# The opening of a hybrid encoder block: latent columns first, one token tile at a time, then the recurrent x branch over all tokens

## The chip, the core and the metric

The kernel runs on one core of a Trainium2 chip. The metric is device time in microseconds (us) of one execution. The engines are TensorE (PE; PEld is its weight load), VectorE (DVE), ScalarE (ACT), GpSimd (POOL) and SyncE (SP), which issues most of the DMAs. A line number such as L475 is a line of the kernel before.

## The reference

One encoder block over 512 tokens of width 1024, in float32. What matters here is its opening:

```python
h = rmsnorm(x, norm1_g)
proj = h @ w_in                    # 1024 x 3488
q_a, kv_a, k_rope_raw = ...        # the first 256 + 128 + 32 = 416 columns: "latent columns"
lru_x, lru_y = ...                 # the next 512 + 512 columns
gate_logits = ...                  # the last 2 x 1024 columns
attn = mla_mixer(q_a, kv_a, k_rope_raw, ...) @ w_o_attn      # both latents go through an RMS norm first
rec = rglru_bidir(lru_x, ...)      # 4-tap convolution, gates from 128x128 blocks, two scans
rec = (gelu(lru_y) * rec) @ w_o_lru
```

The rest (gates, output projection, second norm, SwiGLU of width 2816, last norm) follows and keeps its code but for semaphore counts.

## The kernel before, in words

Every engine has its own instruction list, written out by hand; semaphores order them. Products are made to nearly float32 precision from halves: an operand is rounded to `hi` by ScalarE (`split_hi`, L309) and VectorE subtracts to get `lo` (`split_lo`, L319); `product` (L475 to L477) then issues three matmuls, `lo*hi`, `hi*lo`, `hi*hi`. Weights arrive in two raw buffers (pairs of tiles, `raw`, slots p % 2) and are split into four slots of `w_hi` and `w_lo` (tile t in slot t % 4). A slot is free again when TensorE has counted the tile in `w_used`.

The tiles in order are T_X (four tiles of 128 columns of the recurrent x branch), T_A (four tiles, each two of the eight k-blocks of the 416 latent columns), T_G0 (gate weights of direction 0, two tiles), T_Y (four tiles of 128 columns of the y branch), T_V (values), T_G1 (gates of direction 1), and then the heads.

The opening: SyncE loads token tiles 0 and 1 of x (128 tokens x 1024 each), the first pair of T_X, token tiles 2 and 3, the second pair of T_X, eight small parameter rows, and only then, when slots are free, the latent columns. Tokens are normed in two halves of 256: ScalarE and VectorE make sums of squares, POOL takes the power -1/2 (L616), VectorE scales the rows (L1135), TensorE transposes them (`transpose_half`, L1628), ScalarE and VectorE write `hT_hi` (L729) and `hT_lo` (L1114). For each half of tokens TensorE runs all four T_X tiles with 256 moving columns (`half_tile`). Before that it issues 30 transposes of the identity (L1660) that nothing reads. The second half's 16 transposes come between.

Then follow the latent product (96 matmuls, weights are 128 tokens of `hT`, the moving operand is 416 columns of `w`, token tiles 0 to 3 inside each k-block, into PSUM banks 4 to 7), the convolution on VectorE beside it, the gates of direction 0 (`lru_gates`), two y tiles, 16 transposes of the normed latents (L1711), two more y tiles, the values, the gates of direction 1, `q_and_k(0, 0)` and the loop over heads.

Of the kernel before, what the change touches and what calls it, by code (L numbers as in the profile page):

```python
# [32 lines left out]
P = 128  # L33
ALU = mybir.AluOpType
# [25 lines left out]
T_X, T_A, T_G0, T_Y, T_V, T_G1 = 0, 4, 8, 10, 14, 15  # L60
# [27 lines left out]
def build(nc, x, norm1_g, w_in, q_a_norm_g, w_q_b, kv_a_norm_g, w_kv_b, w_o_attn, conv_w, conv_b,  # L88
# [16 lines left out]
    with ExitStack() as ctx:  # L105
# [33 lines left out]
        nhalf = sb("nhalf", [P, 6])  # L139
# [57 lines left out]
        mse_ready, pow_ready = sem("mse_ready"), sem("pow_ready")  # L197
# [78 lines left out]
        def kind_of(t):  # L276
            if t < T_A or T_Y <= t < T_V:
                return "cols"
            if t < T_G0:
                return "a"  # L280
# [18 lines left out]
        def split_hi(act, t0, dt=0):  # L299
            kind = kind_of(t0)  # L300
            if t0 % 2 == 0:
                act.wait_ge(raw_in[t0 // 2 % 2], dt * (PAIR_INC // 4) + PAIR_INC * (t0 // 4 + 1))
# [9 lines left out]
        def split_lo(dve, t0, dt=0):  # L312
            kind = kind_of(t0)
            dve.wait_ge(w_half, dt + t0 + tiles_in(t0))
# [136 lines left out]
        def gate_bank(d, part, n):  # L451
            return (4 if d != part else 0) + n
# [28 lines left out]
        def _(sync):  # L481
# [14 lines left out]
            def load_lru_x(p):  # L496
                load(p, 0, k_major(p, KD), w_in_v[:, :, C_LX + 256 * p:C_LX + 256 * p + 256])
# [29 lines left out]
            load_lru_gates(4, 0, 0, 32)  # L527
            for p in (5, 6):
                load(p, 0, k_major(p, KD), w_in_v[:, :, C_LY + 256 * (p - 5):C_LY + 256 * (p - 5) + 256])
# [73 lines left out]
        def _(pool):  # L603
# [6 lines left out]
            nc.gpsimd.memset(nhalf[:, 2:4], 1.0).then_inc(s_ident, 1)  # L610
            nc.gpsimd.memset(nhalf[:, 0:2], -0.5).then_inc(s_ident, 1)
# [83 lines left out]
            for count, t, n in ((4, 0, 2), (5, 2, 1), (6, 3, 1)):  # L695
# [5 lines left out]
        def _(act):  # L701
# [30 lines left out]

            act.wait_ge(x_in[0], 16)
            square_sum(xt[:, 0, :], 0, 0, sq_junk[:, 0, :], scale=float(D) ** -0.5)
            act.wait_ge(x_in[1], 16)
            square_sum(xt[:, 1, 0:512], 0, 1, sq_junk[:, 1, 0:512], scale=float(D) ** -0.5)
            split_hi(act, 0)
            act.wait_ge(prm_ready, 1)
            norm_hi(ROW_G1, 4, 0, 0, h_half)
            split_hi(act, 1)  # L740
            for t in (2, 3):
                act.wait_ge(x_in[t], 16)
                square_sum(xt[:, t, :], 0, t, sq_junk[:, t % 2, :])
            split_hi(act, 2)
            split_hi(act, 3)
            norm_hi(ROW_G1, 4, 1, 0, h_half)
# [3 lines left out]
            act.wait_ge(s_pad, 1)  # L750
            for n in range(NB):
                tile_used(act, T_X + n)
                nc.scalar.activation(xp[:, n, LEFT:LEFT + SEQ], ps[:, n, :], ACT.Copy).then_inc(xp_ready, 1)
                split_hi(act, T_A + n)
            for n in range(NB):
                act.wait_ge(xc_full, n + 1)
                nc.scalar.activation(f_hi[:, FXC + n, :], xc[:, n, :], ACT.Copy).then_inc(xc_half, 1)
                if n == 0:
                    split_hi(act, T_G0)
                if n in (2, 3):  # L760
                    split_hi(act, T_Y + n - 2)
# [12 lines left out]

            for t in range(NT):
                act.wait_ge(pa_ready, t + 1)
                square_sum(pa[:, t, 0:QL], 1, t, sq_junk[:, 0, 0:QL])
                square_sum(pa[:, t, QL:QL + KVL], 1, NT + t, sq_junk[:, 1, 0:KVL])
            root(1, 0, 2 * NT, 1)
            gate_sigmoids(0, 1)  # L780
            for t in (T_Y + 2, T_Y + 3, T_V):
                split_hi(act, t)

            act.wait_ge(aT_done, 1)
            for m in range(3):
                act.wait_ge(aT_done, m + 1)
                nc.scalar.activation(f_hi[:, FQA + m, :], ps[:, 4 + m, :], ACT.Copy,
                                     scale=prm[:, ROW_GQ + m:ROW_GQ + m + 1]).then_inc(aT_half, 1)
            act.wait_ge(aT_done, 4)
            nc.scalar.activation(f_hi[NOPE:P, FK, :], ps[NOPE:P, 7, :], ACT.Copy).then_inc(aT_half, 1)  # L790
            split_hi(act, T_G1)
            for m in range(NB):
                tile_used(act, T_Y + m)
                nc.scalar.activation(lru_y[:, m, :], ps[:, m, :], ACT.Gelu_apprx_tanh).then_inc(y_ready, 1)
                if m < 2:
                    split_hi(act, T_HEAD + m)
# [122 lines left out]
            norm_hi(ROW_G2, 0, 1, KD, h2_half)  # L919
# [149 lines left out]
        def _(dve):  # L1069
# [50 lines left out]
            dve.wait_ge(x_in[1], 16)  # L1120
            link(nc.vector.scalar_tensor_tensor(sq_junk[:, 1, 512:D], xt[:, 1, 512:D], 1.0 / D, xt[:, 1, 512:D],
                                                ALU.mult, ALU.mult, accum_out=ssq[:, 0, 4:5]))
            dve.wait_ge(ssq_ready, 1)
            nc.vector.tensor_scalar(mse[:, 0, 0:1], ssq[:, 0, 0:1], EPS, None, ALU.add).then_inc(mse_ready, 1)
            dve.wait_ge(ssq_ready, 2)
            nc.vector.scalar_tensor_tensor(mse[:, 0, 1:2], ssq[:, 0, 1:2], EPS, ssq[:, 0, 4:5], ALU.add,
                                           ALU.add).then_inc(mse_ready, 1)
            for half in range(2):
                if half:
                    dve.wait_ge(ssq_ready, 4)  # L1130
                    nc.vector.tensor_scalar(mse[:, 0, 2:4], ssq[:, 0, 2:4], 1.0 / D, EPS, ALU.mult,
                                            ALU.add).then_inc(mse_ready, 1)
                dve.wait_ge(pow_ready, half + 1)
                for t in (2 * half, 2 * half + 1):
                    nc.vector.tensor_scalar(xt[:, t, :], xt[:, t, :], rstd[:, 0, t:t + 1], None, ALU.mult).then_inc(xn_ready, 1)  # L1135
                split_lo(dve, 2 * half)
                if half:
                    split_lo(dve, 3)
                norm_lo(ROW_G1, 4, half, h_half, h_ready)
                if not half:  # L1140
                    split_lo(dve, 1)
# [6 lines left out]

# [861 lines left out]
```

## Time and profile before

| what | value |
|---|---|
| time, median of 3 runs | 677.28 us (677.25 to 677.99) |
| time of the profiled execution | 679.51 us |
| its span, first to last instruction | 677.7 us |
| TensorE busy in the span | 663.3 us (98%) |
| matmuls | 4006 |

The span is what the trace shows; the profiled execution's own time has 1.8 us around it, and is 2.23 us above the median of the runs. A time in a row is counted from the start of the span. A matmul's own duration is longer than its share of TensorE, since matmuls overlap; the distance from start to start tells the rate.

### The profile page before, as it was taken

How to read it: one execution, taken by the hardware profiler on the slowest of the kernel's cores; microseconds unless marked ns; L12 is line 12 of the kernel's file. 1: busy time of each engine (PE TensorE's matmuls, PEld its weight loads, DVE VectorE, ACT ScalarE, POOL GpSimd, SP SyncE). 2: the span in 40 equal slices, each digit the busy share in tenths (PEclk: the TensorE clock that was granted, in tenths of full speed). 3: DMA queues.
4: the chain of work that ended last, by engine and by line, in shares of the span. 5: the costliest groups of instructions: out<-in, count | busy, mean ns of one | idle time of the engine just before them, and what ended most of it. 6: DMA issues, size and time to landing. Idle time of an engine off the chain costs nothing.

```text
span 677.7 us, 10940 instructions
## 1 busy us (share of the span) xinstructions
PE 663.3 (98%) x4006; PEld 593.1 (88%) x4006; DVE 527.4 (78%) x823; ACT 399.5 (59%) x670; POOL 78.6 (12%) x80
## 2 busy tenths in 40 slices
PE   6999999999999999999999999999999999999996
PEld 6998888888888878888899999999999998778884
DVE  4595647888788886873579997888777769799896
ACT  5436678797777874232565644455554456556573
POOL 1000401011222110000000000000000004304342
PEclk9999999999999999999999999999999999999998
DMA  7324102222222226334062444422444317999903
GB/s 249 122 77 126 54 24 73 69 72 68 62 72 69 103 70 236 120 125 124 3 178 72 125 125 125 112 75 66 120 124 124 124 46 178 238 267 171 171 1 124
DMA packets 83314, 75.94 MB, mean 112 GB/s; under 512 B 6415, under 2 KB 67022, under 8 KB 83278
## 3 DMA queue, kind: packets, MB, share of 16 engines
q1 hardware_dynamic: 77246, 63.93, 31.3%
q0 software_dynamic: 6016, 11.54, 9.5%
q8 instruction: 21, 0.34, 0.2%
q14 instruction: 15, 0.12, 0.1%
q10 hardware_dynamic: 16, 0.00, 0.0%
HBM read 73.37 MB, written 2.10 MB: 111 GB/s over the span
## 4 chain that ended last, share of the span: by engine, by line
PE 80%; DVE 7%; issue 6%; DMA 4%; ACT 2%; POOL 1%; SPq 0%; POOLq 0%; DVEq 0%; ACTq 0%
PE ps L475 15%; PE ps L476 15%; PE ps L477 15%; PE ps L1890 8%; PE ps L1893 8%; PE ps L1892 8%; PE ps L1963 2%; PE ps L1965 2%; PE ps L1967 2%; DMA scr<-in_w_ffn_down_dram 2%; PE ps L1799 2%; DVE w_lo L1389 1%; DMA raw<-in_w_in_dram 1%; DVE f_lo L1384 1%; PE ps L1749 1%
## 5 line engine op out<-in xcount | busy, mean ns | idle before, releaser
L475 PE MATMUL ps<-hT_hi,w_lo 128*128 128x512 f32 (+1 forms) x288 | 100.3, 348 | 3.5 <-DVE hT_lo L1114 3.0
L476 PE MATMUL ps<-hT_lo,w_hi 128*128 128x512 f32 (+1 forms) x288 | 98.6, 342 | 0.0
L477 PE MATMUL ps<-hT_hi,w_hi 128*128 128x512 f32 (+1 forms) x288 | 98.5, 342 | 0.0
L319 DVE TENSOR_TENSOR w_lo<-raw,w_hi 128x1024 fp32r<-128x1024 f32 (+3 forms) x55 | 64.2, 1172 | 36.2 <-ACT w_hi L309 35.1
L1890 PE MATMUL ps<-f_hi,w_lo 128*128 128x256 f32 x320 | 90.7, 283 | 0.0
L1893 PE MATMUL ps<-f_hi,w_hi 128*128 128x256 f32 x320 | 90.6, 283 | 0.0
L1892 PE MATMUL ps<-f_lo,w_hi 128*128 128x256 f32 x320 | 90.6, 283 | 0.0
L309 ACT ACTIVATE w_hi<-raw 128x1024 fp32r<-128x1024 f32 (+3 forms) x55 | 53.8, 987 | 41.1 <-PE ps L477 36.5
L957 ACT ACTIVATE w_hi<-scr 128x1024 fp32r<-128x1024 f32 x50 | 51.9, 1056 | 37.8 <-PE ps L1893 33.4
L1890 PE MATMUL ps<-hT_hi,w_lo 128*128 128x256 f32 x240 | 67.9, 283 | 0.0
L1892 PE MATMUL ps<-hT_lo,w_hi 128*128 128x256 f32 x240 | 67.9, 283 | 0.0
L1893 PE MATMUL ps<-hT_hi,w_hi 128*128 128x256 f32 x240 | 67.9, 283 | 0.0
L475 PEld LDWEIGHTS ps<-hT_hi,w_lo 128*128 128x128 f32 x288 | 54.5, 189 | 11.1 <-DVE w_lo L319 4.0
L1425 DVE TENSOR_TENSOR w_lo<-scr,w_hi 128x1024 fp32r<-128x1024 f32 x50 | 59.5, 1219 | 6.0 <-ACT w_hi L957 5.7
L1890 PEld LDWEIGHTS ps<-f_hi,w_lo 128*128 128x128 f32 x320 | 61.4, 192 | 0.1
L1892 PEld LDWEIGHTS ps<-f_lo,w_hi 128*128 128x128 f32 x320 | 61.4, 192 | 0.0
L1893 PEld LDWEIGHTS ps<-f_hi,w_hi 128*128 128x128 f32 x320 | 61.4, 192 | 0.0
L1963 PE MATMUL ps<-w_hi,f_lo 128*128 128x512 f32 x154 | 60.2, 391 | 1.2 <-DVE f_lo L1384 1.1
L477 PEld LDWEIGHTS ps<-hT_hi,w_hi 128*128 128x128 f32 x288 | 54.5, 189 | 6.4
L1965 PE MATMUL ps<-w_lo,f_hi 128*128 128x512 f32 x154 | 60.0, 389 | 0.0
L1967 PE MATMUL ps<-w_hi,f_hi 128*128 128x512 f32 x154 | 59.9, 389 | 0.0
L476 PEld LDWEIGHTS ps<-hT_lo,w_hi 128*128 128x128 f32 x288 | 54.6, 190 | 5.9
(219 smaller groups left out, 1559.9 us busy)
## 6 DMA issues: line engine op xcount, KB each, us to landing
raw<-in_w_in_dram SPq DMA_DIRECT2D x12, 1024.0 KB
raw<-in_w_ffn_gate_dram SPq DMA_DIRECT2D x12, 512.0 KB, 4.5
raw<-in_w_ffn_up_dram SPq DMA_DIRECT2D x12, 512.0 KB, 5.0
raw<-in_w_ffn_down_dram POOLq DMA_DIRECT2D x12, 512.0 KB, 9.8
scr<-in_w_ffn_down_dram SPq DMA_DIRECT2D x11, 512.0 KB, 8.0
scr<-in_w_ffn_gate_dram SPq DMA_DIRECT2D x10, 512.0 KB, 5.2
scr<-in_w_ffn_up_dram SPq DMA_DIRECT2D x10, 512.0 KB, 5.9
raw<-in_w_out_dram SPq DMA_DIRECT2D x4, 1024.0 KB
```

The lines of the kernel that those rows point to most:

```text
L309: last = nc.scalar.activation(split_view(w_hi, kind, t0 % 4), raw_view(kind, t0 // 2 % 2, t0 % 2), ACT.Copy)
L319: last = nc.vector.tensor_tensor(split_view(w_lo, kind, t0 % 4), raw_view(kind, t0 // 2 % 2, t0 % 2), split_view(w_hi, kind, t0 % 4).bitca ...
L475: nc.tensor.matmul(dst, l_lo, r_hi, start=start, stop=False)
L476: nc.tensor.matmul(dst, l_hi, r_lo, start=False, stop=False)
L477: return nc.tensor.matmul(dst, l_hi, r_hi, start=False, stop=stop)
L1425: nc.vector.tensor_tensor(st_split(w_lo, tile), st_source(par, tile), st_split(w_hi, tile).bitcast(F32), ALU.subtract).then_inc(w_ready, 1)
L1890: nc.tensor.matmul(dst, wl[:, k, :], x_hi[:, k, :], start=start and k == 0, stop=False, skip_group_check=True)
L1892: nc.tensor.matmul(dst, wh[:, k, :], x_lo[:, k, :], start=False, stop=False, skip_group_check=True)
L1893: last = nc.tensor.matmul(dst, wh[:, k, :], x_hi[:, k, :], start=False, stop=k == 3, skip_group_check=True)
L1963: nc.tensor.matmul(dst, f_lo[:, n % 8, tok], w_hi[:, n % 4, col], start=first, stop=False, skip_group_check=True)
L1965: nc.tensor.matmul(dst, f_hi[:, n % 8, tok], w_lo[:, n % 4, col], start=False, stop=False, skip_group_check=True)
L1967: last = nc.tensor.matmul(dst, f_hi[:, n % 8, tok], w_hi[:, n % 4, col], start=False, stop=end, skip_group_check=True)
```

## The change

The tiles are renumbered: T_A comes first (0 to 3), then T_X (4 to 7), and the y tiles are 8, 9, 12 and 13, with T_G0 between them. SyncE loads token tile 0 of x, latent tiles 0 and 1, token tile 1, latent tiles 2 and 3, token tiles 2 and 3; the T_X pairs follow behind the parameter rows and the rope tables, when their raw slots are free. Token tiles are normed one by one: tile 0 as before by ScalarE, VectorE and POOL (half of the squares on each of the first two); for tiles 1 to 3 POOL adds epsilon, takes the power and scales the 1024 columns (`scaled_rows`). POOL also rounds latent tiles 1 to 3 (`a_hi`), which ScalarE did. TensorE runs the latent product token tile by token tile, all eight k-blocks of one token tile in a row, and transposes the next token tile between k-blocks; T_X then runs with 512 moving columns. The idle transposes are 20 and not 30. The latents' norm uses POOL's power in place of ScalarE's square root and VectorE's refinement. PSUM banks and the order of gates, y tiles and values behind the opening are arranged anew: y tile 0, the latents' transposes, y tile 1, gates of direction 0, y tiles 2 and 3, values, gates of direction 1.

```diff
-T_X, T_A, T_G0, T_Y, T_V, T_G1 = 0, 4, 8, 10, 14, 15
+T_A, T_X, T_G0, T_V, T_G1 = 0, 4, 10, 14, 15
+T_Y = (8, 9, 12, 13)
...
 # SyncE
+            def load_a(t):
+                p, j = t // 2, t % 2
+                sync.dma_start(slot(p)[:, 2 * j * CA:2 * j * CA + 2 * CA].rearrange("p (k n) -> p k n", k=2),
+                               w_in_v[:, 2 * t:2 * t + 2, 0:CA]).then_inc(raw_in[p] if j else a_in[p], PAIR_INC if j else 16)
             load_x(0)
+            load_a(0)
+            load_a(1)
             load_x(1)
-            load_lru_x(0)
+            load_a(2)
+            load_a(3)
             load_x(2)
             load_x(3)
-            load_lru_x(1)
...
-            for p in (2, 3):
-                load(p, 0, slot(p)[:, 0:4 * CA].rearrange("p (k n) -> p k n", k=4),
-                     w_in_v[:, 4 * (p - 2):4 * (p - 2) + 4, 0:CA])
...
             sync.dma_start(tab_k[:, :, :, :], rope_k).then_inc(tab_in, 16)
             sync.dma_start(tab_q[:, :], rope_q).then_inc(tab_in, 16)
+            load_lru_x(0)
+            load_lru_x(1)
...
 # POOL
+            def a_hi(t):
+                if t % 2:
+                    pool.wait_ge(raw_in[t // 2], PAIR_INC)
+                else:
+                    pool.wait_ge(a_in[t // 2], 16)
+                nc.gpsimd.tensor_copy(split_view(w_hi, "a", t), raw_view("a", t // 2, t % 2)).then_inc(a_half, 1)
+            def scaled_rows(t):
+                pool.wait_ge(ssq_ready, t + 1)
+                link(nc.gpsimd.tensor_scalar(mse[:, 0, t:t + 1], ssq[:, 0, t:t + 1], EPS, None, ALU.add))
+                link(nc.gpsimd.tensor_tensor(rstd[:, 0, t:t + 1], mse[:, 0, t:t + 1], nhalf[:, 0:1], ALU.pow))
+                nc.gpsimd.tensor_scalar(xt[:, t, :], xt[:, t, :], rstd[:, 0, t:t + 1], None, ALU.mult).then_inc(xs_ready, 1)
+            for t in range(1, 4):
+                a_hi(t)
+            for t in range(1, NT):
+                scaled_rows(t)
...
 # ScalarE
+            square_sum(xt[:, 0, 0:512], 0, 0, sq_junk[:, 0, 0:512], scale=float(D) ** -0.5)
+            split_hi(act, T_A)
             act.wait_ge(prm_ready, 1)
+            h_hi(0)
+            for t in range(1, NT):
                 act.wait_ge(x_in[t], 16)
+                square_sum(xt[:, t, :], 0, t, sq_junk[:, t % 2, :], scale=float(D) ** -0.5)
+                if t > 1:
+                    h_hi(t - 1)
+            h_hi(NT - 1)
+            for n in range(NB):
+                split_hi(act, T_X + n)
...
 # VectorE
+            nc.vector.tensor_scalar(xt[:, 0, :], xt[:, 0, :], rstd[:, 0, 0:1], None, ALU.mult).then_inc(xn_ready, 1)
+            for n in range(4):
+                split_lo(dve, T_A + n)
+                h_lo(0, range(2 * n, 2 * n + 2))
+            nc.vector.sem_inc(w_half, 3)
+            h_lo(1)
+            keep_a(0)
+            h_lo(2)
+            keep_a(1)
+            h_lo(3)
+            keep_a(2)
+            for n in range(3):
+                split_lo(dve, T_X + n)
+            keep_a(3)
+            split_lo(dve, T_X + 3)
...
 # TensorE
-            for n in range(30):
+            for n in range(20):
                 nc.tensor.transpose(ps[:, 6, 0:P], ident[:, :], ident[:, :])
             pe.wait_ge(prm_ready, 1)
+            transpose_rows(0)
+            for t in range(NT):
+                tok = slice(P * t, P * t + P)
+                for k in range(KD):
+                    n, kk = k // 2, k % 2
+                    if not t and not kk:
+                        pe.wait_ge(w_ready, T_A + n + 1)
+                    pe.wait_ge(h_ready, KD * t + k + 1)
+                    last = product(ps[:, t, 0:CA], hT_hi[:, k, tok], hT_lo[:, k, tok],
+                                   split_view(w_hi, "a", n)[:, kk, :], split_view(w_lo, "a", n)[:, kk, :],
+                                   k == 0, k == KD - 1)
+                    if t == NT - 1:
+                        if kk:
+                            used(last)
+                    elif k == KD - 1:
+                        last.then_inc(a_done, 1)
+                    if t < NT - 1 and kk:
+                        if t or n == 3:
+                            transpose_rows(t + 1, (n,))
+                        elif n == 2:
+                            transpose_rows(1, range(3))
+            for n in range(NB):
+                if n == 3:
+                    pe.wait_ge(prm_ready, 2)
+                used(cols_tile(T_X + n, 0, 4 + n))
```

`transpose_rows(t, pairs)` waits until token tile t is scaled (`xn_ready` for tile 0, `xs_ready` for the others), and transposes two 128x128 blocks for each pair. `h_hi` and `h_lo` write `hT_hi` and `hT_lo` of one token tile, eight instructions of 128x128 each; `keep_a` copies one finished token tile of latents out of PSUM.

## Rows read from the trace of the kernel before

**Rows 1.** The page's first part: busy time, share and instructions of each engine.
```profile
PE 663.3 (98%) x4006; PEld 593.1 (88%) x4006; DVE 527.4 (78%) x823; ACT 399.5 (59%) x670; POOL 78.6 (12%) x80
```
**Rows 2.** Waits of TensorE, whole span: total us, times, longest us.
```profile
PE ps L475 <- DVE hT_lo L1114: 3.0, 2, 2.9
...
PE ps L1749 <- DVE f_lo L1291: 1.0, 1, 1.0
PE ps L475 <- DVE w_lo L319: 0.5, 1, 0.5
```
**Rows 3.** Timeline of the opening: start, us, instructions, idle before and releaser.
```profile
2.46 6.20 PE L1660 MATMUL ps<-ident 128*128 128x128 f32 x30
...
4.00 1.06 ACT L715 ACTIVATE scr<-xt 128x1024 f32<-128x1024 f32 x1 [1.12 <-DMA xt<-in_x_dram]
...
6.27 0.70 POOL L616 TENSOR_TENSOR rstd<-mse,nhalf 128x2 f32<-128x2 f32 x1 [3.83 <-DVE mse L1126]
...
10.40 1.06 ACT L309 ACTIVATE w_hi<-raw 128x1024 fp32r<-128x1024 f32 x1 [4.44 <-DMA raw<-in_w_in_dram]
...
13.25 0.35 PE L475 MATMUL ps<-hT_hi,w_lo 128*128 128x256 f32 x1 [2.85 <-DVE hT_lo L1114]
```
**Rows 4.** Windows, by stage: stretch, length, busy time of each engine.
```profile
13.25:39.40 26.15, 25.64 (x209) 25.24 (x210) 18.42 (x33) 13.33 (x26) 0.69 (x1) 1.00 0.26 84
30.67:39.40 8.73, 8.73 (x73) 8.73 (x73) 7.61 (x12) 4.26 (x7) 0.00 (x0) 1.00 0.01 2
39.40:57.52 18.12, 18.12 (x99) 17.95 (x97) 12.22 (x17) 5.58 (x8) 0.00 (x0) 1.00 0.47 146
57.52:97.19 39.67, 39.53 (x183) 32.47 (x181) 24.58 (x64) 30.36 (x56) 7.72 (x5) 1.00 0.19 53
63.46:74.34 10.88, 10.88 (x49) 8.96 (x48) 8.59 (x36) 9.41 (x22) 3.74 (x3) 1.00 0.08 19
...
20.01:21.68 1.67, 1.67 (x19) 1.67 (x17) 1.67 (x2) 0.38 (x2) 0.00 (x0) 1.00 0.60 231
```
**Rows 5.** Timeline of TensorE behind its transposes, and at one pause.
```profile
21.68 0.36 PE L475 MATMUL ps<-hT_hi,w_lo 128*128 128x256 f32 x1
21.88 0.28 PE L476 MATMUL ps<-hT_lo,w_hi 128*128 128x256 f32 x1
...
60.06 0.39 PE L477 MATMUL ps<-f_hi,w_hi 128*128 128x512 f32 x1
60.59 0.50 PE L475 MATMUL ps<-f_hi,w_lo 128*128 128x512 f32 x1
```
**Rows 6.** Windows of the first loads, columns as in Rows 4; GB/s stands last.
```profile
1.00:4.00 3.00, 1.72 (x8) 1.72 (x9) 0.17 (x1) 1.49 (x3) 1.16 (x6) 1.00 0.74 266
4.00:7.00 3.00, 3.00 (x16) 3.00 (x16) 0.92 (x4) 1.87 (x4) 0.70 (x1) 1.00 0.95 309
7.00:10.00 3.00, 3.00 (x24) 3.00 (x24) 1.42 (x2) 0.00 (x0) 0.00 (x0) 1.00 1.04 401
```
**Rows 7.** Groups of POOL's instructions by shape: busy us, mean ns of one.
```profile
L631 POOL TENSOR_TENSOR xt<-xt,store 128x512 f32<-128x512 f32 x4 | 7.5, 1894 | 52.2 <-ACT xt L770 52.2
...
L637 POOL TENSOR_TENSOR store<-store,scr 128x512 f32<-128x512 f32 x4 | 5.2, 1298 | 59.0 <-ACT scr L855 59.0
...
L655 POOL COPY scr<-store 128x512 f32<-128x512 f32 x4 | 2.3, 609 | 5.0 <-DVE store L1309 5.0
L627 POOL CAST f_hi<-scr 128x256 fp32r<-128x256 f32 x5 | 2.0, 398 | 22.9 <-ACT store L770 18.9 <-PE ps L1746 4.0
```
**Rows 8.** Groups of VectorE and ScalarE in the opening by shape, and one timeline row.
```profile
L1114 DVE SCALAR_TENSOR_TENSOR hT_lo<-ps,prm,hT_hi 128x256 fp32r<-128x256 f32 x16 | 6.4, 474 | 0.1
...
L319 DVE TENSOR_TENSOR w_lo<-raw,w_hi 128x832 fp32r<-128x832 f32 x4 | 4.1, 1020 | 0.0
...
L729 ACT ACTIVATE hT_hi<-ps,prm 128x256 fp32r<-128x256 f32 x16 | 6.0, 488 | 2.0 <-PE ps L1628 2.0
...
71.50 5.40 DVE L319 TENSOR_TENSOR w_lo<-raw,w_hi 128x1024 fp32r<-128x1024 f32 x3 [1.78 <-ACT w_hi L309]
```

More of the change, by code:

```diff
@@ L276, in kind_of @@
         def kind_of(t):
-            if t < T_A or T_Y <= t < T_V:
+            if t < T_X:
+                return "a"
+            if t < T_G0 or t in T_Y:
                 return "cols"
-            if t < T_G0:
-                return "a"
             if t == T_V:
@@ L773, in _ @@
             gate_sigmoids(0, 0)
[L775 to L779, printed above, removed]
-            gate_sigmoids(0, 1)
[L781 to L790, printed above, removed]
-            split_hi(act, T_G1)
[L792 to L796, printed above, removed]
+            gate_sigmoids(0, 1)
+            split_hi(act, T_V)
+            split_hi(act, T_G1)
+            gelu(2)
+            split_hi(act, T_HEAD)
+            gelu(3)
+            split_hi(act, T_HEAD + 1)
             gate_sigmoids(1, 0)
@@ L1125, in _ @@
-            dve.wait_ge(ssq_ready, 2)
-            nc.vector.scalar_tensor_tensor(mse[:, 0, 1:2], ssq[:, 0, 1:2], EPS, ssq[:, 0, 4:5], ALU.add,
+            nc.vector.scalar_tensor_tensor(mse[:, 0, 0:1], ssq[:, 0, 0:1], EPS, ssq[:, 0, 4:5], ALU.add,
                                            ALU.add).then_inc(mse_ready, 1)
[L1128 to L1141, printed above, removed]
+            dve.wait_ge(pow_ready, 1)
@@ L1630, in transpose_half, with transpose_rows @@
                             ins.then_inc(xT_done, 1)
+            def transpose_rows(t, pairs=range(KD // 2)):
+                pe.wait_ge(xs_ready if t else xn_ready, t if t else 1)
+                for b in pairs:
+                    for d in (2 * b, 2 * b + 1):
+                        ins = nc.tensor.transpose(x_turned(d), xt[:, t, P * d:P * d + P], ident[:, :])
+                    ins.then_inc(xT_done, 1)
             def half_tile(t0, bank, half, h_sem=None):
@@ L1642, in half_tile @@
                 return last
-            def norm_and_tiles(src, count, base, t0, bank, h_sem):
-                for j in range(4):
-                    half_tile(t0 + j, bank + j, 0, h_sem if not j else None)
-                    if j == 1:
-                        transpose_half(src, count, 1, base)
-                for j in range(4):
-                    used(half_tile(t0 + j, bank + j, 1, h_sem if not j else None))
-                    if j == 0:
-                        pe.wait_ge(prm_in, 16 * 8)
-                        nc.tensor.transpose(ps[:, 7, 0:N_ROWS], rows[0:N_ROWS, :],
-                                            ident[0:N_ROWS, 0:N_ROWS]).then_inc(prm_t, 1)
@@ L1659, in _ @@
-            for n in range(30):
+            for n in range(20):
                 nc.tensor.transpose(ps[:, 6, 0:P], ident[:, :], ident[:, :])
             pe.wait_ge(prm_ready, 1)
-            transpose_half(xt, 0, 0, 4)
-            norm_and_tiles(xt, 0, 4, T_X, 0, h_ready)
-            pe.wait_ge(prm_ready, 2)
-            for n in range(4):
-                t0 = T_A + n
-                pe.wait_ge(w_ready, t0 + 1)
-                wh, wl = split_view(w_hi, "a", t0 % 4), split_view(w_lo, "a", t0 % 4)
-                for kk in range(2):
-                    k = 2 * n + kk
-                    for t in range(NT):
-                        tok = slice(P * t, P * t + P)
-                        last = product(ps[:, 4 + t, 0:CA], hT_hi[:, k, tok], hT_lo[:, k, tok], wh[:, kk, :], wl[:, kk, :],
-                                       k == 0, k == KD - 1)
-                        if k == KD - 1 and t < NT - 1:
-                            last.then_inc(a_done, 1)
-                used(last)
+            transpose_rows(0)
@@ new lines, in _ @@
+            for t in range(NT):
+                tok = slice(P * t, P * t + P)
[17 more added lines that the diff above has]
+                            transpose_rows(1, range(3))
@@ L1679, in lru_gates @@
+            pe.wait_ge(prm_in, 16 * 8)
+            nc.tensor.transpose(ps[:, 7, 0:N_ROWS], rows[0:N_ROWS, :], ident[0:N_ROWS, 0:N_ROWS]).then_inc(prm_t, 1)
+            for n in range(NB):
+                if n == 3:
+                    pe.wait_ge(prm_ready, 2)
+                used(cols_tile(T_X + n, 0, 4 + n))
             def lru_gates(d, t0):
@@ L1717, in _ @@
                 tok = slice(P * t, P * t + P)
[L1718 removed]
+                pe.wait_ge(sig_ready, t + 3)
+                last = product(ps[:, V_BANK[t], :], f_hi[:, FKVA, tok], f_lo[:, FKVA, tok],
                                w_hi[:, T_V % 4, 0:512], w_lo[:, T_V % 4, 0:512], True, True)
```

260 lines of the change are left out of this document (152 added, 108 removed).

## The prediction, made before the change was run

> **What bounds the kernel now.** I read the page's first part first: TensorE is busy for 663.3 of 677.7 us, so only 14.4 us of the span are without a matmul [rows 1]. The next question is where these lie. The waits of TensorE name few: 2.9 us for the first `hT_lo`, 0.5 us for a `w_lo` in the opening, and behind it nothing longer than 1.0 us at a time [rows 2]. So the kernel is bound by TensorE's own list, and a change can gain in two ways: fewer or cheaper matmuls, or an earlier start of the real work. The timeline of the opening shows the start. The first product comes at 13.25 us; the first token tile of x had arrived by 4.00 us, but the weights of T_X only by 10.40 us, when ScalarE had waited 4.44 us for them [rows 3]. The windows by stage then show TensorE without a gap: T_X from 13.25 to 39.40 (26.15 us, the 16 transposes of the second half included), the latent product to 57.52 (18.12 us), the rest to the head loop to 97.19 (39.67 us) [rows 4]. One number is what the change has to beat: T_X and the latent product are both done at 57.52 us.
>
> **Rates.** 96 matmuls of 416 columns in 18.12 us are 0.189 us each; 48 of 512 columns in 10.88 us are 0.227 us; T_X ran 73 of 256 columns in 8.73 us, 0.120 us each; 16 transposes in 1.67 us are 0.104 us [rows 4] (the other counts there hold one to three that overlap the edge). The first matmul behind transposes takes 0.20 us to its follower where the pace is 0.12: 0.08 us for each return from transposes [rows 5].
>
> **The change on TensorE.** The latent product keeps its 96 matmuls: 18.1 us. T_X goes from 192 matmuls of 256 columns to 96 of 512: 96 x 0.227 = 21.8 us, against 26.15 before, of which 1.7 were transposes and about 1.5 the two pauses and the slow first tile. Transposes stay at 32, but 24 of them now stand between products in ten groups: 24 x 0.104 + 10 x 0.08 = 3.3 us. So TensorE's list is hardly shorter; the sum is about the start.
>
> **The start.** Token tile 0 needs all four latent tiles before its eight k-blocks are done, and TensorE's list has, behind the sixth k-block of tile 0, the first transposes of tile 1. Those wait for POOL's `xs_ready`, and everything behind them on TensorE waits too. I call their start T. In front of T on POOL stand, in order, three copies of latent tiles, each behind its load, then add, power and scaling of tile 1.
>
> When does the last latent tile land? The order is x0, a0, a1, x1, a2, a3, sizes 0.524 MB for x and 0.426 for a: its last byte is number 2.75 million. The windows of the loads give 0.80 MB by 4 us, 1.73 by 7, 2.93 by 10 [rows 6]: reached at 9.6 us. Landing is later: x0 by 1.0 us (0.52 MB at about 3.0, used at 4.00), the first T_X pair by 2.5 us (2.10 MB at 7.9, used at 10.40) [rows 3, 6]. That gives 10.6 to 12.1; if the rate of 401 GB/s held from 4 us on, 9.9. I take 11.0, nearer to the short lag, because the long one is that of a load of 1,024 pieces of 1 KB, and a latent tile has 256 pieces of 1.7 KB by its shape.
>
> The copy of 832 columns: 609 ns for 512 and 398 for 256 are 0.82 ns a column, so 0.87 us [rows 7]. POOL's product took 1.89 us in the stretch in which VectorE subtracted, 1.30 elsewhere; at that ratio the copy takes 1.3, my high end. Add and power: the power of two columns took 0.70 [rows 3], of one I expect no more, and I put the add and two handovers at 0.2: 0.9 (0.7 at least). POOL's scaling of 1024 columns has no row. Below it stands the copy's rate, 1.03 us; above it two two-input products of 512 columns at 1.30, 2.6 us [rows 7]. It has one tensor input as the copy has, so I take 1.3. T = 11.0 + 0.87 + 0.9 + 1.3 = 14.1 us; with all low ends 12.5, with all high ends 16.9.
>
> Other work in front of T is covered. The squares of x0 and the power come as early as before [rows 3]; VectorE then needs 1.0 us for each latent tile's `lo` and at most 0.8 for two `hT_lo` [rows 8], which leaves it waiting for the loads. If ScalarE's square of x2, which stands in front of `h_hi(1)`, came late by its load (3.28 MB, about 13.4 us at worst, and 1.1 for the square), products of tile 1 are not due before T + 2.2 = 16.3.
>
> Behind T TensorE has work without a pause, if the helpers keep up: 24 transposes 2.5, ten returns and that of the parameter rows' transpose with it 1.0, the last two k-blocks of tile 0 and three whole tiles, 78 x 0.189 = 14.7, T_X 21.8: 40.0 us. A token tile is 5.4 us on TensorE with its transposes. ScalarE needs at most 8 x 0.38 plus a square of 1.06, VectorE at most 8 x 0.40 plus a copy of under 1.0 [rows 3, 8], POOL 1.9 to 3.5 us: all less. On SyncE's queue the T_X loads stand behind the parameter rows and wait until latent tiles are split, about 14 us for the second pair; at the slowest window's 266 GB/s 1.05 MB take 4 us each, so both are there by some 22 us [rows 6]. They are needed from T + 13: the T_X weights are split during tile 3, whose k-blocks free the slots at 1.13 us each, about as fast as ScalarE (1.06) and VectorE split them, and T_X spends 5.4 us on each. So T_X ends at 14.1 + 40.0 = 54.1 us, not 57.52: 3.4 us gained.
>
> **Behind the opening** the same matmuls follow as in 57.52 to 97.19. The pause at 60.06 (0.53 to the next start where the pace is 0.23) is a gate that waits for VectorE's first latent copy [rows 5]; latents are now copied long before: 0.3 us more. y tile 0 (5.4 us) hides the convolution of the last x block, y tile 1 hides the splitting of the latents; ScalarE's gelus and sigmoids have 5 us tiles beside them. I put the new table changes and banks at nothing, since ScalarE is busy for only 30.36 of 39.67 us in this stretch [rows 4]; uncovered, one wait would cost a us. Longer waits than 1.0 us are absent later [rows 2], so the heads and the SwiGLU should move up whole. The power in place of square root and refinement is off TensorE's path.
>
> **The sum** is -3.4 - 0.3 = -3.7 us. The profiled execution took 679.51, so 675.8 like for like; it lay 2.23 us above the median of the runs, 677.28, so the predicted median is 673.6.
>
> **One rule against it.** In the stretch of POOL's slow products VectorE's three subtractions took 1.80 us each for 1024 columns, 1.02 being the time for 832 in the opening [rows 8]. The Trainium skill (GPSIMD Engine Reference, Specifications) says that GpSimd shares its SBUF interfaces with VectorE and contends with VectorE instructions that have two SBUF inputs; the rows agree. By that rule POOL's last copy, which meets VectorE's subtraction of the tile before, takes the high end of 1.3 us: 674.0.
>
> **Rivals.** (a) POOL is the new wait, and T comes at its late end: loads land at 12.1, copies contend, scaling runs at the two-input rate. T = 16.9 gives 57.52 - 56.9 + 0.3 = 0.9 us: 676.4, no measurable change. For it: three unknown rates in one chain. Against: one tensor input. 0.09.
>
> (b) It is hidden: an engine behind the opening takes the gain back, and the head loop begins when it did: 677.3. Against it stand the short waits [rows 2]. 0.05.
>
> (d) POOL's first scaling starts late, as TensorE waits for it. From 5.1 us on that makes the kernel slower. POOL's first copies and casts show no such lateness in their means [rows 7]: 0.03. The Trainium skill (GPSIMD Engine Reference, Instruction dispatch) puts the first call of a freshly loaded kernel at about 6 us, which would be 679.6 here; no row shows it.
>
> **Numbers.** The forecast has 0.76, and is faster. No change (within 0.2%, 1.35 us, about what a measurement here can tell): 0.09 + 0.05 + 0.04 = 0.18. Slower: 0.03 + 0.03 = 0.06. The range runs from T = 12.5 with half of the returns free, 2.0 us below the forecast, or 671.5 rounded, to rival (a) and the short clock case, 676.5.
>
> **What would show it.** Right: first product near 8 us, a pause of TensorE that ends with POOL's scaling near 14 us, T_X ending near 54, the head loop starting near 93.5. Wrong: a wait for `xs_ready` again at tiles 2 or 3 (POOL slower than 5.4 us a tile), matmuls of 416 columns at 0.38 us (clock), or new TensorE waits between 54 and 94 us.

## The result: 679.0 us, slower by a quarter of a per cent

The changed kernel takes 679.0 us (median of 13 runs, 678.34 to 680.64) beside 677.64 us for the kernel before on the same chip (13 runs, 676.62 to 678.64): a ratio of 1.0025, interval 1.0017 to 1.0033. The forecast was 673.6 us with a range of 671.5 to 676.5. It was wrong in sign and by 5.4 us.

The profiled execution took 678.77 us with a span of 676.9. Its page begins as before's does [rows 1]: TensorE is busy for 98%, now with 106 matmuls fewer.

```profile
PE 662.3 (98%) x3900; PEld 587.0 (87%) x3900; DVE 528.9 (78%) x827; ACT 399.2 (59%) x681; POOL 94.2 (14%) x94
```

The waits of TensorE (total us, times, longest us) show what replaced the 2.9 us in front of the first product [rows 2]:

```profile
PE ps L1709 <- POOL xt L663: 3.8, 1, 3.8
...
PE ps L490 <- DVE hT_lo L1187: 1.0, 2, 0.5
PE ps L1832 <- DVE f_lo L1364: 0.9, 1, 0.9
```

The timeline of TensorE in the opening (start, us, instruction, idle before) shows the first product at 8.66 us, where before had 13.25 [rows 3]. Three pairs of k-blocks of token tile 0 are done by about 13.3; then TensorE stands until POOL has scaled token tile 1.

```profile
8.66 0.43 PE L490 MATMUL ps<-w_hi,hT_lo 128*128 128x416 f32 x1 [0.54 <-DVE hT_lo L1187]
...
12.97 0.34 PE L492 MATMUL ps<-w_hi,hT_hi 128*128 128x416 f32 x1
17.11 1.08 PE L1709 MATMUL ps<-ident,xt 128*128 128x128 f32 x6 [3.79 <-POOL xt L663]
...
18.33 0.55 PE L491 MATMUL ps<-w_lo,hT_hi 128*128 128x416 f32 x1
18.68 0.55 PE L492 MATMUL ps<-w_hi,hT_hi 128*128 128x416 f32 x1
...
21.13 0.35 PE L492 MATMUL ps<-w_hi,hT_hi 128*128 128x416 f32 x1
21.32 0.35 PE L490 MATMUL ps<-w_hi,hT_lo 128*128 128x416 f32 x1
...
36.16 0.27 PE L1749 MATMUL ps<-ident,rows 63*128 63x63 f32 x1
36.36 0.50 PE L490 MATMUL ps<-hT_hi,w_lo 128*128 128x512 f32 x1
```

From 18.33 to 18.68 is 0.35 us for a matmul of 416 columns, and from 21.13 to 21.32 it is 0.19: behind the pause TensorE runs at about half the rate, the 1.2 GHz level. The windows by stage (length, busy time of PE, PEld, DVE, ACT, POOL, granted clock, DMA share, GB/s) say so too: granted clock 0.57 in the stretch behind the pause, 0.99 to 1.00 after it.

```profile
13.32:17.11 3.79, 0.01 (x1) 0.01 (x1) 0.54 (x3) 0.00 (x0) 3.54 (x3) 1.00 1.09 350
17.11:20.84 3.73, 3.73 (x16) 3.51 (x16) 1.64 (x6) 1.76 (x7) 3.52 (x3) 0.57 0.59 188
20.84:36.16 15.32, 15.32 (x88) 14.59 (x87) 9.12 (x23) 9.55 (x23) 3.77 (x4) 0.99 0.00 1
36.16:58.27 22.11, 22.11 (x98) 18.26 (x98) 19.19 (x39) 9.70 (x27) 2.16 (x3) 1.00 0.40 120
58.27:97.44 39.17, 39.17 (x183) 32.56 (x181) 22.61 (x43) 26.80 (x40) 6.86 (x5) 1.00 0.19 54
```

T_X ends at 58.27 us (57.52 before) and the head loop starts at 97.44 (97.19 before) [rows 4]. In the pause of 3.79 us POOL works for 3.54, VectorE for 0.54 and ScalarE not at all. POOL's timeline, and VectorE's beside it, show the chain that TensorE waits for:

```profile
9.60 0.88 POOL L656 CAST w_hi<-raw 128x832 fp32r<-128x832 f32 x1 [1.38 <-DMA raw<-in_w_in_dram]
10.67 1.61 POOL L656 CAST w_hi<-raw 128x832 fp32r<-128x832 f32 x1 [0.19 <-DMA raw<-in_w_in_dram]
12.38 1.06 POOL L661 TENSOR_SCALAR mse<-ssq 128x1 f32<-128x1 f32 x1
13.53 0.56 POOL L662 TENSOR_TENSOR rstd<-mse,nhalf 128x1 f32<-128x1 f32 x1
14.19 2.86 POOL L663 TENSOR_SCALAR xt<-xt,rstd 128x1024 f32<-128x1024 f32 x1
17.13 0.22 POOL L661 TENSOR_SCALAR mse<-ssq 128x1 f32<-128x1 f32 x1
...
18.11 2.86 POOL L663 TENSOR_SCALAR xt<-xt,rstd 128x1024 f32<-128x1024 f32 x1
```
```profile
10.52 1.03 DVE L327 TENSOR_TENSOR w_lo<-raw,w_hi 128x832 fp32r<-128x832 f32 x1 [0.30 <-POOL w_hi L656]
...
12.32 1.03 DVE L327 TENSOR_TENSOR w_lo<-raw,w_hi 128x832 fp32r<-128x832 f32 x1 [0.25 <-POOL w_hi L656]
13.26 0.60 DVE L1187 SCALAR_TENSOR_TENSOR hT_lo<-ps,prm,hT_hi 128x128 fp32r<-128x128 f32 x2
18.24 1.64 DVE L1187 SCALAR_TENSOR_TENSOR hT_lo<-ps,prm,hT_hi 128x128 fp32r<-128x128 f32 x6 [4.38 <-ACT hT_hi L789]
```

The scaling takes 2.86 us, while VectorE does nothing from 13.86 to 18.24; so this is POOL's own rate, and the next tile's takes 2.86 too. The last copy takes 1.61 us where the one before took 0.88, and adding epsilon to one column takes 1.06 where the next tile's takes 0.22. Both slow ones lie beside a subtraction of VectorE.

### The profile page after: what moved, and what is told of

It reads as the page before. It is cut to its first block, busy times and chain, and to the rows that moved or that the text cites. A ratio compares the mean times of both kernels' runs of the same rounds, so it can differ in the third digit from the quotient of the medians.

```text
span 676.9 us, 10760 instructions
## 1 busy us (share of the span) xinstructions
PE 662.3 (98%) x3900; PEld 587.0 (87%) x3900; DVE 528.9 (78%) x827; ACT 399.2 (59%) x681; POOL 94.2 (14%) x94
## 4 chain that ended last, share of the span: by engine, by line
PE 91%; DVE 3%; issue 1%; DMA 1%; ACT 1%; POOL 1%; SPq 0%; POOLq 0%; DVEq 0%; ACTq 0%
PE ps L490 15%; PE ps L492 15%; PE ps L491 15%; PE ps L1973 10%; PE ps L1975 10%; PE ps L1976 10%; PE ps L2046 4%; PE ps L2050 4%; PE ps L2048 4%; PE ps L1882 2%; DVE w_lo L1462 1%; PE ps L1832 1%; DMA raw<-in_w_in_dram 1%; PE ps L1829 1%; DVE f_lo L1457 1%
## 5 line engine op out<-in xcount | busy, mean ns | idle before, releaser
L490 PE MATMUL ps<-hT_hi,w_lo 128*128 128x512 f32 (+1 forms) x256 | 94.2, 368 | 0.2 <-DVE hT_lo L1178 0.2
L492 PE MATMUL ps<-hT_hi,w_hi 128*128 128x512 f32 (+1 forms) x256 | 93.0, 363 | 0.0
L491 PE MATMUL ps<-hT_lo,w_hi 128*128 128x512 f32 (+1 forms) x256 | 92.9, 363 | 0.0
L314 ACT ACTIVATE w_hi<-raw 128x1024 fp32r<-128x1024 f32 (+3 forms) x52 | 51.3, 991 | 20.9 <-PE ps L492 20.2
L731 POOL DMA_DIRECT2D raw<-in_w_ffn_down_dram x12 | 14.7, 1223 | 344.3 <-DVE w_lo L1462 344.3
L490 PEld LDWEIGHTS ps<-hT_hi,w_lo 128*128 128x128 f32 x256 | 48.3, 189 | 8.5 <-issue 0.6
L492 PEld LDWEIGHTS ps<-hT_hi,w_hi 128*128 128x128 f32 x256 | 48.3, 189 | 7.6
```

The lines of the kernel that those rows point to most:

```text
L490: nc.tensor.matmul(dst, l_lo, r_hi, start=start, stop=False)
L491: nc.tensor.matmul(dst, l_hi, r_lo, start=False, stop=False)
L492: return nc.tensor.matmul(dst, l_hi, r_hi, start=False, stop=stop)
```

## Experiments

My theory after the result: POOL's chain to the scaled tile 1 is the whole cause, for its rates and because VectorE's subtractions hold it up; the pause that it makes costs TensorE its clock on top. Rivals: POOL pays for the first use of an instruction; the clock alone is the loss; or something behind the opening takes the gain.

**VectorE scales tiles 1 to 3.** POOL keeps the addition and the power.

```diff
-                link(nc.gpsimd.tensor_tensor(rstd[:, 0, t:t + 1], mse[:, 0, t:t + 1], nhalf[:, 0:1], ALU.pow))
-                nc.gpsimd.tensor_scalar(xt[:, t, :], xt[:, t, :], rstd[:, 0, t:t + 1], None, ALU.mult).then_inc(xs_ready, 1)
+                power(rstd[:, 0, t:t + 1], mse[:, 0, t:t + 1], 1, pow_ready)
...
+            def scale_rows(t):
+                dve.wait_ge(pow_ready, t + 1)
+                nc.vector.tensor_scalar(xt[:, t, :], xt[:, t, :], rstd[:, 0, t:t + 1], None, ALU.mult).then_inc(xs_ready, 1)
...
+            scale_rows(1)
+            scale_rows(2)
             h_lo(1)
             keep_a(0)
+            scale_rows(3)
```

> VectorE and not POOL scales the 1024 columns of token tiles 1 to 3; POOL still adds and takes the power. If POOL's chain sets the start T of tile 1's transposes (17.1 us after the change), T comes at about 14.9 us (power done near 14.1, 0.75 us of scaling), the pause of TensorE shrinks from 3.8 to about 1.7 us, the clock stays up, and T_X ends near 54.9 us, not 58.3: a median near 675.3 us. If the engines behind the opening give the time back anyway, T_X ends early but the head loop still starts near 97 us and the median stays near 679. If the clock alone were the loss, T would move and only the 1.2 us at the lower level come back: 677.5.

Measured: 675.69 us, ratio to before 0.9984, interval 0.9976 to 0.9993. In VectorE's timeline the scaling takes 0.75 us, and in TensorE's the transposes of tile 1 start at 15.08 (17.11), with a pause of 1.59 us and full rate behind it:

```profile
14.27 0.75 DVE L1210 TENSOR_SCALAR xt<-xt,rstd 128x1024 f32<-128x1024 f32 x1 [0.25 <-POOL rstd L637]
```
```profile
15.08 0.88 PE L1716 MATMUL ps<-ident,xt 128*128 128x128 f32 x6 [1.59 <-DVE xt L1210]
...
15.98 0.35 PE L491 MATMUL ps<-w_lo,hT_hi 128*128 128x416 f32 x1
16.18 0.35 PE L492 MATMUL ps<-w_hi,hT_hi 128*128 128x416 f32 x1
...
93.82 0.44 PE L490 MATMUL ps<-hT_hi,w_lo 128*128 128x512 f32 x1
```

The head loop starts 3.6 us earlier than in the changed kernel: 2.0 by the earlier transposes, 1.6 because no matmul behind them is slow (78.74 us from the transposes to the head loop, 80.33 in the changed kernel). So POOL's chain, with the slow matmuls behind its pause, was the loss, and nothing behind the opening ate the gain. The clock is not quite safe yet: eight of the runs took 675.00 to 675.76 us at 0.997 to 0.999, four took 676.83 to 677.85 at 0.992 to 0.996.

**The pause filled.** 34 idle transposes stand in front of tile 1's, so that TensorE works through the wait.

```diff
                         elif n == 2:
+                            for _ in range(34):
+                                nc.tensor.transpose(ps[:, 3, 0:P], ident[:, :], ident[:, :])
                             transpose_rows(1, range(3))
```

> The changed kernel with 34 transposes of the identity (nothing reads them) in TensorE's pause before tile 1's transposes; POOL's chain is untouched. If the pause lets the clock fall, T stays at 17.1 us, the matmuls behind it run at 0.19 and not 0.35 us, T_X ends near 57.0 us, and the two clusters of runs of the changed kernel (about 678.6 and 680.2) become one near 677.4 us. If the two clusters have another cause, the spread of 2 us stays, and the median stays within 0.5 us of 679.0.

Measured: 678.48 us, ratio 1.0019, interval 1.0010 to 1.0028; granted clock 0.997 to 0.999 in all 11 runs. In TensorE's timeline the transposes still start at 17.13, the matmuls behind run at 0.19 us at once, and a second wait appears:

```profile
17.13 0.88 PE L1709 MATMUL ps<-ident,xt 128*128 128x128 f32 x6
...
18.04 0.35 PE L491 MATMUL ps<-w_lo,hT_hi 128*128 128x416 f32 x1
18.22 0.35 PE L492 MATMUL ps<-w_hi,hT_hi 128*128 128x416 f32 x1
...
21.05 0.44 PE L1709 MATMUL ps<-ident,xt 128*128 128x128 f32 x2 [0.56 <-POOL xt L663]
...
96.66 0.45 PE L490 MATMUL ps<-hT_hi,w_lo 128*128 128x512 f32 x1
```

The clock is restored and the kernel is still slower than before: the clock is a part of the loss, not the whole. It gave back 0.8 us at the head loop (96.66, and 97.44 in the changed kernel), and the median came down to 678.48, not to the 677.4 that I expected. With TensorE at full rate POOL's scaling of tile 2 becomes late in its turn, by 0.56 us; in the changed kernel the slow stretch hid that. POOL's three steps for a tile take 3.9 us from one scaling to the next (14.19 and 18.11 in the changed kernel), and TensorE at full rate comes from the first transposes of tile 1 to those of tile 2 in 3.2 us (15.08 to 18.27 in the experiment before).

**An early call.** POOL adds epsilon to a spare column before the opening's work.

```diff
+            link(nc.gpsimd.tensor_scalar(mse[:, 0, 4:5], nhalf[:, 0:1], EPS, None, ALU.add))
             pool.wait_ge(mse_ready, 1)
             power(rstd[:, 0, 0:1], mse[:, 0, 0:1], 1, pow_ready)
```

> The changed kernel with one more tensor_scalar of one column on POOL, in its idle time near 2.5 us, whose result nothing reads. If the 1.06 us of POOL's first one-column tensor_scalar (0.22 for the later ones) is a price of the first call, the one at 12.4 us now takes 0.22, T comes 0.84 us earlier at 16.3, and the median is 0.8 us lower, more if the pause of 2.9 us no longer lets the clock fall (677 to 678.2). If it was contention in that place, T and the median stay: 17.1 and 679.0.

Measured: 679.13 us, ratio 1.0026, interval 1.0017 to 1.0035. The early call takes 0.25 us at 2.53, the one that counts still 1.05 at 12.73, and the scaling 2.87; the transposes of tile 1 start at 17.46. Rival (d) falls with the changed kernel's own rows: POOL's first scaling starts 0.10 us behind the power and takes 2.86 us, as the second does. No first use costs anything that these rows show.

**The changed kernel once more**, for the spread.

> The changed kernel once more, on the chip of the others, as the level to compare with: 679.0 us with runs in two clusters; its profile shows either a lower-clock stretch of about 3.7 us behind the pause, or, if it falls in the upper cluster, one that is about twice as long, if the clock makes the clusters.

Measured: 679.32 us, ratio 1.0024, interval 1.0011 to 1.0037. In this profile TensorE is back at 0.19 us a matmul at 21.97 us instead of 21.13, 4.9 us behind the start of the transposes instead of 4.0, and the head loop starts at 98.10 instead of 97.44. So the slow stretch is longer, but not twice as long, and it accounts for 0.66 of the 0.9 us between the two spans (676.9 and 677.8). The runs sort by granted clock: 677.54 us at 0.999 (one run), 678.5 at 0.995, 679.01 to 680.11 at 0.992. That the length of the slow stretch makes the rest of the spread too is likely, but only these two executions have a profile; and why the one run at 0.999 is faster than all runs with the filled pause is not shown.

**The kernel before once more.**

> The kernel before, unchanged, for a second profiled execution of it. If the first profile of before is a typical execution, the head loop starts again near 97.2 us and the span is near 677.7 us. If that execution was a long one (its own time was about 2 us above the median), the span is near 675.4 us, and the missing 2 us show either in the opening (head loop near 95.5 to 96.5 us) or in the last phase of the kernel (about 1.4 us shorter than in the first profile).

Measured: 677.62 us with a span of 675.8. Its timeline of TensorE:

```profile
12.24 0.36 PE L475 MATMUL ps<-hT_hi,w_lo 128*128 128x256 f32 x1 [1.72 <-DVE hT_lo L1114]
...
96.15 0.45 PE L475 MATMUL ps<-hT_hi,w_lo 128*128 128x512 f32 x1
```

All of it stands 1.0 us earlier than in the first profile of before (13.25 and 97.19) [rows 3, 4], and what follows the head loop's start is 0.9 us shorter (675.8 - 96.15 = 579.65, against 677.7 - 97.19 = 580.5). The execution from which I forecast had a long opening and a long end; its first weights were used from 10.40 us on, here from 9.38. Against 96.15 the changed kernel's head loop is 1.3 us late, and 1.95 in its second profile, near what the medians say (1.4 and 2.2 us).

**ScalarE rounds the fourth latent tile.** POOL's last copy is taken out of the chain; VectorE's subtraction of that tile then waits for ScalarE.

```diff
-            for t in range(1, 4):
+            for t in range(1, 3):
                 a_hi(t)
...
 # ScalarE, behind the square of tile 1
+                if t == 1:
+                    act.wait_ge(raw_in[1], PAIR_INC)
+                    nc.scalar.activation(split_view(w_hi, "a", 3), raw_view("a", 1, 1), ACT.Copy).then_inc(a_last, 1)
```

> The changed kernel with the rounding of the fourth latent tile moved from GpSimd to ScalarE, so that GpSimd is free for the mean's addition from about 10.7 us on. The scaling of tile 1 then runs from about 12.2 us, beside VectorE's subtraction of the fourth latent tile. If GpSimd's 2.86 us for 1024 columns is its own rate and only the copies and additions lost time to VectorE, the transposes of tile 1 start at about 15.2 us (17.1 in the changed kernel). If the scaling also stops for the length of VectorE's subtraction with two inputs, it takes 3.4 to 3.9 us and they start at about 16.0 us. The pause of TensorE shrinks from 3.8 us to about 2 to 3 us; if it is the length of the pause that takes the clock down, the slow matmuls behind it go too, and the time falls by 2 to 3 us against the changed kernel (about 676 to 677 us); if they stay, by about 1 to 2 us (677 to 678 us).

Measured: 677.46 us (676.21 to 680.39), ratio 1.0002, interval 0.9989 to 1.0015: no change against before. In the profiled execution the gain on T can't be read, since its loads came late (POOL's first copy starts at 8.49 us, 7.26 in the changed kernel) and T is 16.98. But POOL's timeline, and VectorE's, show the scaling beside a subtraction:

```profile
13.59 3.33 POOL L665 TENSOR_SCALAR xt<-xt,rstd 128x1024 f32<-128x1024 f32 x1
...
17.98 2.86 POOL L665 TENSOR_SCALAR xt<-xt,rstd 128x1024 f32<-128x1024 f32 x1
```
```profile
13.18 1.01 DVE L329 TENSOR_TENSOR w_lo<-raw,w_hi 128x832 fp32r<-128x832 f32 x1
```

3.33 against 2.86: 0.47 us more, for an overlap of 0.60 (13.59 to 14.19). And the pause shrank to 1.41 us, yet the clock was low all the same: TensorE's timeline has 0.35 us from start to start already at 13.63, behind pauses of 1.26 and 0.95 us with only six matmuls between them.

```profile
10.83 0.42 PE L492 MATMUL ps<-w_hi,hT_lo 128*128 128x416 f32 x1 [1.26 <-DVE hT_lo L1192]
...
13.15 0.68 PE L492 MATMUL ps<-w_hi,hT_lo 128*128 128x416 f32 x1 [0.95 <-DVE hT_lo L1192]
13.63 0.55 PE L493 MATMUL ps<-w_lo,hT_hi 128*128 128x416 f32 x1
13.98 0.55 PE L494 MATMUL ps<-w_hi,hT_hi 128*128 128x416 f32 x1
```

By the granted clock it isn't so in every execution: the three runs with a granted clock of 0.999 took 676.21 to 676.59 us, the four at 0.994 to 0.995 took 677.23 to 678.21, the three at 0.992 to 0.993 took 678.43 to 680.39. By this measure the slow matmuls went away in three runs of ten.

**VectorE's subtractions held back.** Nothing with two SBUF inputs runs on VectorE until POOL has scaled tile 1.

```diff
             for n in range(4):
+                if n == 2:
+                    dve.wait_ge(xs_ready, 1)
                 split_lo(dve, T_A + n)
                 h_lo(0, range(2 * n, 2 * n + 2))
```

> The changed kernel, with VectorE's subtractions for the third and fourth latent tile held back until GpSimd has scaled tile 1 of x, so that nothing with two SBUF inputs runs on VectorE beside GpSimd's last copy and the mean's addition. Theory (GpSimd stands still while such a subtraction runs): the third copy takes 0.88 us as the first two do (1.61 in the changed kernel), the one-column addition 0.22 us (1.06), the scaling 2.86 us as before, and it ends near 15.5 us instead of 17.05. Rival (the copy and the addition are slow for a reason of their own, as the load that still runs or the handover): 1.6 and 1.06 us stay, and it ends near 17. The time isn't the point here: the held-back subtractions make the products of tile 0 late, so no gain is expected (677 to 680 us).

Measured (one run): 680.26 us. POOL's timeline, and the two subtractions in VectorE's:

```profile
10.65 0.89 POOL L656 CAST w_hi<-raw 128x832 fp32r<-128x832 f32 x1 [0.17 <-DMA raw<-in_w_in_dram]
11.63 0.25 POOL L661 TENSOR_SCALAR mse<-ssq 128x1 f32<-128x1 f32 x1
...
12.63 2.86 POOL L663 TENSOR_SCALAR xt<-xt,rstd 128x1024 f32<-128x1024 f32 x1
15.58 1.06 POOL L661 TENSOR_SCALAR mse<-ssq 128x1 f32<-128x1 f32 x1
...
17.39 3.34 POOL L663 TENSOR_SCALAR xt<-xt,rstd 128x1024 f32<-128x1024 f32 x1
```
```profile
15.53 1.02 DVE L327 TENSOR_TENSOR w_lo<-raw,w_hi 128x832 fp32r<-128x832 f32 x1 [5.45 <-POOL xt L663]
...
16.99 1.01 DVE L327 TENSOR_TENSOR w_lo<-raw,w_hi 128x832 fp32r<-128x832 f32 x1
```

The copy is back at 0.89 us, the addition at 0.25, and tile 1 is scaled at 15.49 instead of 17.05. The subtractions moved, and the slowness moved with them, to the next addition (1.06) and the next scaling (3.34). This settles it: beside a subtraction that began before it a POOL instruction stands. The addition that began at 15.58 ended at 16.64, 0.09 us behind the subtraction's end at 16.55; in the changed kernel it was 13.44 and 13.35. And the loss follows the overlap, not the length of the POOL instruction: the copy met the subtraction for 0.88 us and lost 0.73, the addition 0.97 and 0.84, the scaling 0.61 and 0.48 (0.60 and 0.47 in the experiment before), each 0.13 to 0.15 us less than the overlap.

**A constant for the factor.** Is it the factor's column, as a second input, that makes the scaling slow?

```diff
-                nc.gpsimd.tensor_scalar(xt[:, t, :], xt[:, t, :], rstd[:, 0, t:t + 1], None, ALU.mult).then_inc(xs_ready, 1)
+                nc.gpsimd.tensor_scalar(xt[:, t, :], xt[:, t, :], 0.5, None, ALU.mult).then_inc(xs_ready, 1)
```

> The changed kernel, with GpSimd multiplying the token tiles 1 to 3 by a constant in place of the per-row factor; this leaves the norm's factor out of these tiles. If it is the factor's column, read beside the tile, that makes the scaling run at the rate of products with two inputs, 1024 columns take 1.1 to 1.3 us here as a copy's do, tile 1 of x is ready near 15.4 us and the time falls by 1 to 2 us against the changed kernel. If it is the multiplication itself, 2.8 us stay, and nothing changes.

Measured (one run): 679.87 us, and POOL's timeline has

```profile
14.60 2.81 POOL L663 TENSOR_SCALAR xt<-xt 128x1024 f32<-128x1024 f32 x1
```

2.81 and then twice 2.79 us: the multiplication itself costs it, not the column that the factor comes from. What in this instruction is slow stays open.

**All together.** VectorE scales, with tile 1 ahead of its subtraction of the fourth latent tile, and ScalarE rounds that tile, by the edits above and this one, against the first experiment's kernel:

```diff
             for n in range(4):
+                if n == 3:
+                    scale_rows(1)
                 split_lo(dve, T_A + n)
                 h_lo(0, range(2 * n, 2 * n + 2))
             nc.vector.sem_inc(w_half, 3)
-            scale_rows(1)
+            h_lo(1, range(4))
             scale_rows(2)
-            h_lo(1)
+            h_lo(1, range(4, KD))
             keep_a(0)
             scale_rows(3)
```

> VectorE scales the token tiles 1 to 3 (as in the earlier run of that), the fourth latent tile is rounded by ScalarE, and the scaling of tile 1 stands ahead of VectorE's subtraction of the fourth latent tile. If the opening is set by the chain from x's tile 1 to its transposes, these start near 13.2 us instead of 15.1, with TensorE's pause all but gone; the head loop starts near 92.5 us (93.8 with VectorE's scaling alone, 97.4 in the changed kernel) and the median falls to about 674.4 us. If the opening is by then set by something behind that chain (the lower halves of the hidden tiles, the scaled rows of tiles 2 and 3, the loads), the gain shows at the start of tile 1's products but not at the head loop, and the time stays at 675.7 us.

Measured: 673.77 us (673.59 to 674.28), ratio 0.9948, interval 0.9934 to 0.9961; granted clock 0.997 to 0.999. TensorE's timeline has no pause in front of tile 1's transposes and one of 0.41 us behind them, and the window from there to the head loop is 79.36 us:

```profile
13.57 0.36 PE L494 MATMUL ps<-w_hi,hT_hi 128*128 128x416 f32 x1
13.76 0.84 PE L1722 MATMUL ps<-ident,xt 128*128 128x128 f32 x6
15.01 0.43 PE L492 MATMUL ps<-w_hi,hT_lo 128*128 128x416 f32 x1 [0.41 <-DVE hT_lo L1191]
```
```profile
13.76:93.12 79.36, 78.95 (x382) 67.48 (x381) 55.03 (x114) 47.79 (x95) 11.18 (x12) 1.00 0.29 85
```

The new order is worth 3.6 us when token tile 1 is ready by the time TensorE asks for it: 3.0 at the head loop (93.12, and 96.15 in the second profile of before), and 0.6 behind it (672.2 - 93.12 = 579.1, against 579.65). That this time is near the forecast's 673.6 is in part luck: its tile 1 is ready by another way, and the forecast's errors behind T and in the base, told below, go opposite ways.

## Why the prediction was wrong

**The step that failed is T**, the start of tile 1's transposes: 17.11 us where I had 14.1, beyond my own late end of 16.9. The sum had a wrong size for POOL's scaling and no price for what VectorE does to a small POOL instruction. By its terms:

| term | forecast | measured |
|---|---|---|
| last latent tile at POOL | 11.0 | 10.67 |
| its copy | 0.87 (high end 1.3) | 1.61 |
| from there to the scaling | 0.9 | 1.91 |
| scaling of 1024 columns | 1.3 (bounds 1.03 to 2.6) | 2.86 |

The scaling is half of the miss. "One tensor input as the copy has" was the wrong likeness: with the column and with the constant alike, POOL's multiplication goes at 2.7 to 2.8 ns a column, near the two-input product's 2.5 (1.30 us for 512 columns) and far from the copy's 1.06 (0.88 us for 832). I had the product's row and put it at the far end [rows 7].

**The rule that I weighed was right, and I charged too little for it.** I let contention with VectorE stretch one copy by half and add 0.4 us. In the changed kernel it cost 0.73 us on the copy and 0.84 on the addition, which I had put, with two handovers, at 0.2 us and free of contention. In these rows a POOL instruction that meets a running subtraction does not slow down in proportion; it waits until the subtraction ends, however short it is itself. The Trainium skill (SBUF — State Buffer, SBUF: two separate sides) says just this: of the two engines the one that starts first has the shared pair of ports for its whole instruction, and the other blocks fully. The held-back subtractions bear that out, with ends 0.09 us apart.

**Rival (a) came, and brought (c) with it.** I gave POOL's late end 0.09 and the clock 0.07, as separate cases. But a late T is a pause of TensorE, and with the pause filled the slow matmuls were gone. The 2.85 us pause in before [rows 3], which I held against (c), stood behind 46 transposes without a break and left the rate at full; 3.79 us behind 18 matmuls in three groups with gaps did not. The short case of (c) had 5.6 us of work at the low level and 2.8 us lost; no row gave the 5.6. The runs showed slow stretches that end 4.0 and 4.9 us behind T. From T to the head loop it is 80.33 and 81.0 us in the two profiles of the changed kernel, against 78.74 where VectorE scales and no matmul is slow, so the clock cost 1.6 to 2.3. The two parts overlap: with the clock restored and POOL as it was, only 0.8 to 1.4 us came back at the head loop (96.66, and 97.44 and 98.10), in part because tile 2 was then late. "POOL 1.9 to 3.5 us: all less" compared POOL with a whole token tile on TensorE, 5.4 us, where the first transposes of tile 2 come 3.2 us behind T and POOL needs 3.9.

**The base was 1.0 us too long.** I took the 57.52 us, at which T_X and the latent product are done, from an execution whose opening was that much later than in the second profile, and then subtracted 2.23 us for the same lateness in the whole. With 96.15 in place of 97.19 the forecast head loop of 93.5 is worth 2.7 us, not 3.7. The ledger: T 3.0, clock 1.6 to 2.3, base 1.0, less 0.7 for the work behind T, which is shorter than I had it (next paragraph): 4.9 to 5.6 together; the miss was 5.4.

**What was right.** From T to the head loop I had 40.0 + 39.4 = 79.4 us; it is 78.74 where VectorE scales, and 79.36 in the best version, with waits of 0.4 us for `hT_lo` and the like in it. T_X took 22.11 us in the changed kernel, the parameter rows' transpose included (forecast 21.8). The first product came at 8.66 (near 8), the loads when estimated (10.67 for 11.0). The pause at 60.06 is gone: 39.17 us from T_X to the head loop, where 39.67 became 39.4 in the forecast. The new gates, banks and table changes cost nothing that TensorE's waits show.

## What to carry to other kernels

Price an instruction on POOL by what it does and not by its number of inputs, and look at what VectorE runs at that moment: a one-column addition in a chain that TensorE waits for can cost as much as the two-input instruction that VectorE has just begun (1.06 us beside one of 1.03 here). A long wait on TensorE and a fall of its clock are to be priced together, since here the first brought the second. And where the profiled execution is 2 us off the median, find the stage in which these lie before that stage's length goes into the sum.

## What was unexpected of the hardware

- POOL's multiplication of 128x1024 float32 by a column took 2.86 us, by a constant 2.79 to 2.81; VectorE's took 0.75. The Trainium skill (GPSIMD Engine Reference, Engine selection) calls one-input work on GpSimd roughly line-rate; that fits the copy (0.88 us for 832 columns), and not these.
- A one-column addition on POOL took 0.22 to 0.25 us away from VectorE's two-input work, 0.93 to 1.06 beside a subtraction, and 0.78 beside VectorE's own scaling, which has one tensor input.
- TensorE's rate fell behind a pause of 3.79 us, and in one execution behind pauses of 1.26 and 0.95 with thin work between, while pauses of 0.57, 0.97 and 0.41 in the best version's profile, and one of 1.59 where VectorE scales, left it at full. The filled pause shows that the 3.79 us mattered; what decides with shorter pauses, and in a given execution, stays open, since no kernel here varied that alone.
